# Four places for expert groups in each router head of a two-layer diffusion backbone

## What is computed

```python
q = (x @ wq).reshape(N, PEER_HEADS, 2, PEER_DKEY // 2)           # queries, two halves
s = jnp.einsum('nhpd,hpkd->nhpk', q, keys)                        # scores against 128 keys each
top_s, top_i = lax.top_k(s, K)                                    # best 16 of each half
cand = top_s[:, :, 0, :, None] + top_s[:, :, 1, None, :]
best_s, best = lax.top_k(cand.reshape(N, PEER_HEADS, K * K), K)   # best 16 of 256 sums
expert = (i1 * PEER_NKEYS + i2)                                   # i1, i2: the indices behind best
gate = jax.nn.softmax(best_s, axis=-1)
a = gelu(einsum('tkd,td->tk', u_tab[expert], x)); y = einsum('tk,tkd->td', gate * a, v_tab[expert])
```

## Time and profile before

| | us |
|---|---|
| median of 3 runs (5910.4 to 5916.87) | 5913.59 |
| the profiled execution, device time | 5908.96 |
| its span, first to last instruction | 5906.8 |
| PE busy | 4106.9 (70%) |
| DVE busy | 2900.1 (49%) |
| ACT busy | 1711.8 (29%) |
| POOL busy | 1440.7 (24%) |
| gathers, share of the 16 DMA engines | 56.9% |

### The profile page before, as it was taken

How to read it: one execution, slowest core, us unless ns; L and a number is a source line. 1 busy time by engine, 2 the same in 40 slices (tenths; PEclk the granted TensorE clock), 3 DMA queues, 4 the chain that set the end, 5 groups by cost and what they waited for, 6 DMA issues and landing times.

```text
span 5906.8 us, 63901 instructions
## 1 busy us (share of the span) xinstructions
PE 4106.9 (70%) x22248; PEld 2491.4 (42%) x22248; DVE 2900.1 (49%) x6835; ACT 1711.8 (29%) x4745; POOL 1440.7 (24%) x1295
## 2 busy tenths in 40 slices
PE   3889577889886686447566677778556888545555
PEld 1678454566564343214223234667223555311111
DVE  0321747544447544764444443421676444754444
ACT  0200137332432442233222222200224253222222
POOL 0000012222221232223344441000222222135443
PEclk7779789979997898779788888759778899767777
DMA  6434367748896798669899995114777799589998
GB/s 254 157 126 163 127 232 296 284 175 323 318 359 234 284 412 361 265 247 400 352 412 415 403 413 233 54 45 163 309 300 302 302 371 369 217 321 421 405 419 355
DMA packets 259315, 1712.65 MB, mean 290 GB/s; under 512 B 37712, under 2 KB 39344, under 8 KB 71600
## 3 DMA queue, kind: packets, MB, share of 16 engines
q0 software_dynamic: 184320, 1342.26, 56.9%
q1 hardware_dynamic: 74672, 366.31, 16.8%
HBM read 1690.43 MB, written 17.92 MB: 289 GB/s over the span
## 4 chain that ended last, share of the span: by engine, by line
PE 44%; DMA 23%; DVE 14%; ACT 6%; DVEq 4%; issue 4%; POOL 3%; ACTq 2%; SPq 1%; PEld 0%; PEldq 0%; POOLq 0%
PE psum L436 26%; DMA arena<-in_uv,arena 19%; PE psum L787 10%; DVE arena L2033 3%; POOL arena L1121 3%; DVE arena L1945 1%; DVE arena L1938 1%; DMA arena<-in_w_ada 1%; DVE arena L1939 1%; PE psum L396 1%; PE psum L617 1%; PE psum L618 1%; ACT arena L1457 1%; ACT arena L1216 1%; DMA arena<-in_w_mix 1%
## 5 line engine op out<-in xcount | busy, mean ns | idle before, releaser
L1121 POOL DMA_INDIRECT arena<-in_uv,arena x1280 | 1436.8, 1123 | 4430.0 <-PE psum L787 2999.4
L787 PE MATMUL psum<-arena 64*64 64x512 f32 x10240 | 1572.2, 745 | 1146.8 <-ACTq L1458 1061.0
L2033 DVE CUSTOM_DVE_ANT_0 arena<-arena 128x1024 f32<-128x1024 f32 x1280 | 1550.6, 1226 | 1258.0 <-DMA arena<-in_uv,arena 1198.2
L436 PE MATMUL psum<-arena 128*128 128x256 f32 (+2 forms) x8480 | 1943.4, 387 | 120.5 <-DVEq L1477 78.5
L436 PEld LDWEIGHTS psum<-arena 128*128 128x128 f32 (+1 forms) x8480 | 1613.8, 194 | 545.9 <-issue 178.5
L787 PEld LDWEIGHTS psum<-arena 64*64 64x64 f32 x10240 | 395.4, 158 | 2137.2 <-ACTq L1458 1414.4
L1451 ACT ACTIVATE arena<-arena 128x2 f32<-128x2 f32 x640 | 130.9, 205 | 1735.6 <-DVEq L2035 1725.1
L1457 ACT ACTIVATE arena<-arena 128x64 f32<-128x64 f32 x1280 | 376.1, 340 | 46.1 <-issue 2.1
L396 PE MATMUL psum<-arena 128*128 128x128 f32 (+1 forms) x680 | 128.0, 343 | 314.6 <-DVE arena L1536 121.6
L1454 ACT ACTIVATE arena<-arena 128x1 f32<-128x1 f32 x1280 | 307.7, 287 | 45.8 <-issue 1.7
L1897 DVE TENSOR_TENSOR arena<-arena,psum 128x256 f32<-128x256 f32 x120 | 50.6, 422 | 436.6 <-ACT arena L1371 434.5
(11 more groups left out here) (210 smaller groups left out, 2730.0 us busy)
## 6 DMA issues: line engine op xcount, KB each, us to landing
arena<-in_w_in SPq DMA_DIRECT2D x92, 1024.0 KB, 6.3
arena<-in_w_mix SPq DMA_DIRECT2D x120, 768.0 KB, 7.2
arena<-in_w_ada SPq DMA_DIRECT2D x32, 1536.0 KB, 16.4
arena<-in_w_wq SPq DMA_DIRECT2D x40, 1152.0 KB, 5.9
arena<-in_w_wo SPq DMA_DIRECT2D x20, 1024.0 KB, 7.6
arena<-in_uv,arena POOLq DMA_INDIRECT x1280, 11.9
arena<-ada_rows SPq DMA_DIRECT2D x15, 512.0 KB, 5.7
arena<-x_rows SPq DMA_DIRECT2D x14, 512.0 KB, 7.1
```

What stands on the lines that cost most here:

```text
L436: ins = mm(out, a, b, start=(i == 0), stop=(i == last))
L787: ins = mm(psum[o, r_ * 512:r_ * 512 + 512], DIAG[rows, c, :], RING[rows, sl, D + half * 512:D + (half + 1) * 512], start=first, stop=last ...
L1121: pool.indirect_dma_start(RING[:, sl, :], None, io["uv"], bass.IndirectOffsetOnAxis(IDX[:, t, h * TOPK + k:h * TOPK + k + 1], 0)).then_inc ...
L2033: V_.tensor_tensor_reduce(out=RING[:, sl, 0:D], in0=RING[:, sl, 0:D], in1=XT[:, u % 2, :], scale=1.0, scalar=0.0, op0=ALU.mult, op1=ALU.ad ...
```

## The change

A router's head has four places instead of one. On DVE they lie behind the first `top16`, behind the second, behind the combination, and at the head's end. PE and ACT do a quarter of a head's queries or scores before each: scores of the second half of head h; queries of head h+1, first half; second half; scores of the first half of head h+1. Ahead of the first head PE now makes only the queries of head 0 and its first scores, where it made the queries of heads 0 and 1. ACT's softmax of head h-1 stands in the third quarter. SP yields four times a head. `steps` gives 4 places of 5.0 a head (20, before 12), and in the router of layer 1, pair 1, 4 of 7.0 (28, as before).

```diff
     if kind == "route":
-        return [(28.0 if (l, pairs) in FIRST_ROUTES else 12.0)] * PH
+        return [(7.0 if (l, pairs) in FIRST_ROUTES else 5.0)] * (4 * PH)
...
-                if st[0] == "route" and n < PH - 1:
-                    want = max(done, min(want, routed_upto(items, st[1], st[2], n)))
+                if st[0] == "route" and n < 4 * PH - 1:
+                    want = max(done, min(want, routed_upto(items, st[1], st[2], max(0, (n + 1) // 4 - 1))))
...
-                queries(0)
+                queries(0, 0)
+                queries(0, 1)
+                scores(0, 0)
                 for h in range(PH):
+                    scores(h, 1)
+                    yield
                     if h + 1 < PH:
-                        queries(h + 1)
-                    scores(h)
+                        queries(h + 1, 0)
+                    yield
+                    if h + 1 < PH:
+                        queries(h + 1, 1)
+                    yield
+                    if h + 1 < PH:
+                        scores(h + 1, 0)
                     yield
...
                 for h in range(PH):
                     chunks(1)
-                    yield
+                    for _ in range(4):
+                        yield
...
                         dve.drain().then_inc(s("top"), 1)
+                        yield
...
                     dve.drain().then_inc(s("best"), 1)
+                    yield
```

More of the change, by code:

```diff
@@ L743, in route, with queries, scores @@
                 w_at = {}
-                def queries(h):
-                    w_at[h] = weights(l, "wq", h)
+                def queries(h, pp):
+                    if pp == 0:
+                        w_at[h] = weights(l, "wq", h)
                     w = view(w_at[h], [KD, PW])
[L748 to L752, removed]
+                    (b,) = fill(("q", l, p, 2 * h + pp))
+                    full(chain(bank(b, PW), [(w[:, k, pp * P:(pp + 1) * P], ht[:, k, :]) for k in range(KD)]))
+                def scores(h, pp):
                     keys = view(w_at[h] + 2048, [2, P])
[L754 to L761, removed]
-                queries(0)
+                    (b,), _, (f,) = UNIT["q", l, p, 2 * h + pp]
+                    pe.wait_ge(bank_out[b], f + 1)
+                    (b,) = fill(("s", l, p, 2 * h + pp))
+                    for i in range(2):
+                        ins = mm(bank(b)[:, i * P:(i + 1) * P], qst[:, 2 * (h % 2) + pp, i * P:(i + 1) * P], keys[:, pp, :], start=True, stop=True)
+                    full(ins)
+                    if pp:
+                        weights_done()
+                queries(0, 0)
+                queries(0, 1)
+                scores(0, 0)
                 for h in range(PH):
+                    scores(h, 1)
+                    yield
                     if h + 1 < PH:
-                        queries(h + 1)
-                    scores(h)
+                        queries(h + 1, 0)
[5 more added lines that the diff above has]
+                        scores(h + 1, 0)
                     yield
@@ L1397, in route, with queries, scores @@
                 act.wait_ge(s("x1_out"), nxt("x1_out", 32))
-                def queries(h):
+                def queries(h, pp):
                     if h >= 2:
                         act.wait_ge(s("filled"), UNIT["s", l, p, 2 * h - 3][1])
-                    for pp in range(2):
-                        (b,) = whole(("q", l, p, 2 * h + pp))
-                        empty(A.activation(qst[:, 2 * (h % 2) + pp, :], bank(b, PW), ACT.Copy), b)
+                    (b,) = whole(("q", l, p, 2 * h + pp))
+                    empty(A.activation(qst[:, 2 * (h % 2) + pp, :], bank(b, PW), ACT.Copy), b)
+                def scores(h, pp):
+                    n = 2 * h + pp
+                    (b,) = whole(("s", l, p, n))
+                    if n >= 2:
+                        act.wait_ge(s("top"), cnt["top"] + n - 1)
+                    empty(A.activation(sco[:, pp, :], bank(b, PW), ACT.Copy), b)
                 def softmax(h):
@@ L1410, in softmax @@
                     act.drain().then_inc(s("best_exp"), 1)
-                queries(0)
+                queries(0, 0)
+                queries(0, 1)
+                scores(0, 0)
                 for h in range(PH):
+                    scores(h, 1)
+                    yield
                     if h + 1 < PH:
[L1415 to L1421, removed]
+                        queries(h + 1, 0)
+                    yield
                     if h:
                         softmax(h - 1)
-                    if h == PH - 1:
+                    if h + 1 < PH:
+                        queries(h + 1, 1)
+                    yield
+                    if h + 1 < PH:
+                        scores(h + 1, 0)
+                    else:
                         softmax(h)
```

## The result

The changed kernel takes 5717.39 us (median of 4 runs, 5712.05 to 5721.4), before 5913.59 us (median of three); the ratio is 0.9673, 95% interval 0.9659 to 0.9687. One run of the kernel before (6156.57 us) and one of the last experiment (14741 us) took far longer than the others; medians and ratios leave both out, and their cause is open. That is 3.3% faster, where 2.5% was forecast: 5717 against 5763, inside the range. The profiled executions are 5908.96 and 5714.84 us, 194 apart.

A forecast was written before the change was run, and what follows sets the result against it. No engine bounds the whole: gathers bound the tail, PE or transfer the merges, DVE, with waits for scores, the routers. Terms -7 - 12 - 48 + 15 - 24 - 50 - 16 - 1 - 8 = -151 gave 5763 us, range 5705 to 5860.

The forecast's parts named there:

- the five starts: Starts of the five routers: PE does one head's queries first instead of two heads', each start 7.1 us shorter.
- R2: Router R2 with 48 groups: 36.5 us a head plus start and end, 305 us; +15, bounds -9 and +47.
- The merge: Merge of pair 2: 9 groups fewer at 5.3 us each, -48 us; at PE's 2.0 it would be -18.
- the context: Context of layer 1: 6 groups fewer at 4 us each, -24 us, bounds -12 and -32.
- the dense stages of units 0 and 1: R1's segment: 8 groups leave stages where PE is busy, at 1.95 us each, -15.6 us.
- R3: Router R3: bursts of 8, 7 and 5 groups, later heads spread; 296 us, before 347: -50, bounds -26 and -62.
- The stages between R3 and R4: Stages up to and including the merge of pair 2, layer 1: 3 groups fewer each, -16 us, bounds -12 and -24.
- The tail's 8 us: Tail: unit 8's tokens are loaded in R4, so the 8.29 us wait goes and gathers follow: -8 us.
- PE at its lower clock: Rival, chance 0.18: in the routers PE's halves between waits run at the lower clock; 5806 to some 5815 us.
- Less from the groups moved: Rival, chance 0.11: merge gives 2.0 us a group and context 1.95, their sum 42 us smaller: 5805 us.
- The change not doing what it says: Rival, chance 0.08: PE holds scores behind a group whose gather has not landed; 70 to 87 us of waits stay: 5840.
- The ring: Rival, chance 0.07: slot rounds limit the spread groups in R2, R3, R4; a 34 us round uses up the gain.

The follow-up runs named there:

- the last experiment: Changed kernel with at most two groups a place in the routers and 6.0 instead of 5.0 as a place's cost: 5685.12 us (median of five), ratio 0.9616.
- the ring experiment: Changed kernel with six slots in the ring of gathers, three groups under way, instead of eight and four: 6164.22 us, ratio 1.0428.
- the run with the late load: Changed kernel with the tokens of unit 8 loaded at its own group 0 again, as before the change: 5716.15 us, ratio 0.9676.

## Why the prediction was right, and where it was off

The mechanism held in its main parts. DVE's waits for scores fell from 176.2 to 55.4 us, the five starts, where some 55 was forecast. R2 and R4 took 15 and 10 groups more in no more time. The merge became shorter by 6.3 us for each of its nine groups, the context by 5.5 for each of six (forecast 5.3 and 4), the dense stages of units 0 and 1 by 2.4 for each of eight (1.95). Not all of that is the groups' own: against the run with new places and old counts it is 53 us for the merge, 5.9 a group, and 30 for the context, 5.0 a group.

**The term that was mis-sized is R2.** The floors in the sum were 271 us for DVE and 281 for the transfer, and I took 305, 36.5 a head, since two engines near full on the same stretch "will not fit without gaps" (8 x 36.5 and the 11 us of start and end are 303, by the way). Measured are 32.5 to 33.7 a head, and 41.2 for the one with a unit's end, so R2 lasts 287 us from its first matmul to the end of its last group: 18 less than forecast, and within 6 of the larger floor. The step that failed is the allowance for gaps of some 4 us a head: DVE waited 13.9 us for gathers in all of R2. The estimate from the ring experiment, four groups served every 4.7 us, would say why none was needed, but that is argued and not shown. The other 12 of the term's 31 us are not the allowance: my window of R2 before ended at 2625, but the last burst of four groups ran on to 2632.8, 8 us; and the load of tokens between that point and the next norm took 11.4 us before and takes 6.8 now, 5 us that no term had.

**Smaller ones.** R3 is -58 for -50, but the stage itself was forecast well, 296 for the 294 measured. Its bound before was wrong: the window began at 4135, the first matmul at 4129.7. Within the stage errors cancel: the last three spread heads take 32.6, 32.5 and 30.0 us, not 34, while the heads with the bursts of 8 and 7 take 53.0 and 51.4, not 51.3 and 49.7 (by the step of the rows a burst of 8 costs 35, not the 34 of the sum). The stages between R3 and R4 gave 6 instead of 16, 1 us a group where 2.54 and 2.8 were taken; against the run with old counts they gave 10. Why it is less than PE's own 1.95 a group no run shows. The tail's 8 us were wrong in kind: 8.29 us of DVE waiting lay on the chain of the profile, but the run with the late load puts the early one at nothing that can be measured, since the next gather waits for PE there and not for the tokens.

**Why the waits go.** The prediction argued from the new order, by which PE's scores stand ahead of what DVE needs. The runs show that this is one of two causes, each of which is nearly enough by itself. Spreading alone leaves 28 us of waits at the later heads, the order alone less than one. The order's own share in the changed kernel is 57 us, 35 of them at the starts.

**The rivals.** PE at its lower clock: the granted clock went up, from 0.74 to 0.81 in R2 and from 0.75 to 0.82 in R4, and most half queries (29 of the 42 that have a row of their own in R1 to R4) took 3.6 to 3.8 us, none 7. Single groups on PE fell to the lower level more often: of R2's 38 that have a row of their own, 21 took 1.95 us and 14 took 3.4 to 3.7. DVE's heads of R2 stayed at 33 us all the same. Two groups on PE in the same head of R2, behind 1.78 and 5.71 us of idle time:

```profile
2316.18 1.95 PE L796 MATMUL psum<-arena 64*64 64x512 f32 x16 [1.78 <-ACTq L1478]
...
2324.48 3.69 PE L796 MATMUL psum<-arena 64*64 64x512 f32 x16 [5.71 <-ACTq L1478]
```

The rule of the Trainium skill (TensorE: Matmul & The Clock Gate, HAM oscillation) that short bursts between waits start at the low rate holds for the second of these; the first, and the half queries shown above, kept the upper level. Less from the groups moved: they brought more. The change not doing what it says: DVE's waits at later heads are gone. The ring: four groups take at most some 22 us in R2, not 34. What I had not seen is that half of the change by itself, the counts without the places, is 55 us slower.

## What to carry to other kernels

Where engines run in fixed orders a few items apart, a burst longer than that distance turns the next dependent step into a wait (here bursts of three at a distance of two, some 9 us each time), and a burst longer than the ring turns it into a wait for transfers. Cut the long step into pieces and put one or two items between, and both waits shrink together. Move work into a stage only after its bursts are gone: the same shift cost 55 us before and gave 38 after (5755 to 5717). Where two engines are both near full, the larger of their two floors can be the better forecast than that floor with an allowance for gaps: R2 came within 6 us of it, but that is one stage of one kernel. Set the bounds of a stage by its instructions, and the same way before and after: two windows that were a few microseconds off made 13 us of the difference between forecast and result.

## What was not expected of the hardware

DVE at 83% busy and the DMA engines at a share of 0.98 ran side by side for 290 us with no stretching of either: two groups in a row still begin 2.54 us apart on DVE (2320.49 and 2323.03), and the DMA engines moved 395 GB/s, as in the tail. With three groups under way instead of four, they moved 346 GB/s in the tail and 337 in R2.
